# RWKV-7 mixer on one core: keys and bonus moved into the edge of a round, triangle and centring product placed later on TensorE, and the scan's state update made by ScalarE instead of VectorE

## The chip, the cores and the metric

The kernel runs on one core of one Trainium2 chip. The metric is the device time of one execution in microseconds (us), as the median of several runs. The engines are TensorE (PE in the views; PEld is its weight load), VectorE (DVE), ScalarE (ACT), GpSimd (POOL) and SyncE (SP, which issues the DMAs). Each works through its own queue in order, and they wait for one another by semaphores.

## What is computed

The program is the trunk of an encoder with two layers, 512 tokens and a width of 1024. Each layer has a token mixer (four heads of latent attention and eight heads of a bidirectional RWKV-7 recurrence, merged by one output projection) and a gated MLP. The change touches only the recurrence and what stands around it:

```python
def step(state, inp):
    r_t, w_t, k_t, v_t, kk_t, a_t = inp
    sa = jnp.einsum('bhvk,bhk->bhv', state, -kk_t)
    state = (state * w_t[:, :, None, :]
             + sa[..., None] * (kk_t * a_t)[:, :, None, :]
             + v_t[..., None] * k_t[:, :, None, :])
    y = jnp.einsum('bhvk,bhk->bhv', state, r_t)
    return state, y
...
def direction(xw, xa, d, reverse):
    w = rwkv_decay(xw, w0[d], w2[d])
    a = jax.nn.sigmoid(a0[d] + xa @ a2[d])
    k_d = k * (1 + (a - 1) * k_a)
    y = wkv7_scan(heads(r), heads(w), heads(k_d), heads(v), kk, heads(a), reverse)
    return y, k_d
...
y = y_f + y_b
mu = jnp.mean(y, axis=-1, keepdims=True)
var = jnp.mean(jnp.square(y - mu), axis=-1, keepdims=True)
y = ((y - mu) * lax.rsqrt(var + GN_EPS)).reshape(B, S, W) * gn_g + gn_b
k_bonus = 0.5 * (k_f + k_b)
bonus = jnp.sum(heads(r * k_bonus) * r_k, axis=-1, keepdims=True) * heads(v)
return (y.astype(r.dtype) + bonus.reshape(B, S, W)) * g
```

## The kernel before

The eight recurrent heads are worked in four blocks of two heads. A layer has five rounds (`rwkv_round`, called with cur = -1 to 3). Three blocks are in hand at a time. The round of block `cur` **scans** it; it **builds** block `cur + 1`, which means inverting its 64 x 64 triangular chunk matrices; it **trails** block `cur - 1`, which is the group norm, the gate and the bonus; and it prepares block `cur + 2` **early**, with its decays and rates. This text calls the four rounds that scan round 0 to round 3. Round 0 scans, builds and prepares, round 1 does all four, round 2 does everything except prepare, and round 3 scans and trails. Layer 0 has its scans at about 331 to 507 us of the span, layer 1 at about 1237 to 1412 us.

The 512 tokens of a block are 8 chunks of 64, and both time directions and both heads go together. So the scan has 8 **steps**, s = 0 to 7, each one passing from engine to engine and back:

- TensorE multiplies the state into the right side (`scan_state`, L640, then the reads L644 and the carry of the state L646, where the identity matrix copies it into the bank in which the update is added).
- ScalarE copies the right side out of PSUM (also named `scan_state`, L1103). Behind it comes the copy of the next chunk's tokens (`scan_ring`, L1098).
- TensorE **solves** with the inverse (`scan_solve`, L656), and then multiplies the Gram matrices of a later chunk (L603) and the values (L625).
- ScalarE copies the solution (`scan_solve`, L1110, two instructions of 64 partitions each).
- TensorE makes the state product (`scan_update`, L666) and the outputs (L672), and transposes the tokens of a later chunk (L615 to L618).
- VectorE multiplies the state product by the chunk's decay and writes the new state (`scan_state`, L1602). The next step's L640 waits for it.

```python
            def scan_state(it, s):

                dve.wait_ge(sc_p.sem, sc_p.at(f"S{s}", it))
                own(sc_v, TTT(SM[(s + 1) % 2], PS[1][:, 2 * P:3 * P].rearrange("p (d v) -> p d v", d=2),
                              EM[it % 2][:, :, s].unsqueeze(2).to_broadcast([P, 2, C]), ALU.mult), f"S{s}")
```

The order of each queue is written out by hand in the three functions `rwkv_round`, one for each engine, by the number of the step. The lists of step names (`sc_p`, `sc_a`, `sc_v`) turn a name into a semaphore value.

- TensorE has, at step 0, the second triangle of the block being built (L530, ahead of the state product) and the centring product of the trailing block (L680); at step 2 the variance product (L685), at step 3 the bonus product (L540), at step 4 the next block's decay product (L516), and at step 6 (step 4 in round 3) the gate (L690). The 512-wide ones each take TensorE for about the same time.
- ScalarE has, behind the solution copy of its step: the triangle copies (L1052, step 0); one inverse copy (L1061) and a table load with the square and the copy of the centred block (L961, L1123, L1124, step 1); the reversed values (L1045, step 2); a logarithm (L1133, step 3); three inverse copies (L1067, L1069, step 4); the next block's tanh (L1013, step 5); the norm's factor (L1138, step 6, in round 3 step 4) and the shift of the decays (L1019, step 6). In round 3 pairs of output copies (L1128) stand at steps 0, 2 and 5.
- VectorE has, behind the state update of its step, the masking of the Gram matrices (`scan_ring`, L1596) and a piece of the inverse. At step 0 both halves of `keys` (L1472 and L1474) and the inverse's transpose (L1507), at step 1 `bonus` (L1478, L1480), at step 4 `bonus_end` (L1485), at step 7 the group norm's end (`tail_norm`, L1609 to L1613), the decay sums (L1445) and the end of the inverse (L1575, L1577, L1585).

Between two scans lies the **edge**: the inverse is transposed and completed on TensorE and ScalarE in a chain of short products and copies (`rwkv_level`, L561 to L580, and `level`), while VectorE prepares the block after the next one (`queries`, `removals`). TensorE enters the edge only when VectorE's last reduction of the inverse (L1575) is done.

## Time and profile before

| | |
|---|---|
| median of 3 runs | 1866.26 us (1866.06 to 1869.93) |
| profiled execution: its time | 1867.6 us |
| profiled execution: its span | 1865.7 us |
| TensorE busy, share of the span | 1652.5 us, 89% |
| TensorE weight load | 1213.6 us, 65% |
| VectorE | 1007.7 us, 54% |
| ScalarE | 732.9 us, 39% |
| GpSimd | 289.4 us, 16% |
| mean granted TensorE clock | 0.939 |

The shares are means over stages with different limits. The chain of waits that ended last lies 57% on TensorE, 26% in TensorE's issue and other waits for nothing visible, 8% on VectorE and 4% on ScalarE. Outside the scans most of the span is TensorE's three-product matrix multiplications (L500 to L502). The clock is given as a share of the full 2.4 GHz: 1.00 is full speed, about 0.5 is the lower level of 1.2 GHz. In the timeline, times count from the start of the span; a bracket says how long the engine had stood idle before the instruction and for whom.

### The profile page before, as it was taken

The numbers are of one execution on the slowest core, as the hardware profiler recorded it, in microseconds if no ns is written. First come the engines' busy times: TensorE is split into PE (matmuls) and PEld (weight loads), VectorE is DVE, ScalarE is ACT, GpSimd is POOL, SyncE is SP. The second block draws the span as 40 slices with busy tenths as digits, with TensorE's granted clock in tenths as the row PEclk, the third lists the DMA queues.
The fourth block names the chain that finished last, engine by engine and source line by source line (L and its number), as shares of the span: only waits on it lengthen the run. The fifth ranks groups of instructions, "written<-read, shape, count | busy, mean of one in ns | idle before, by whom it ended". The sixth has DMA issues, their size and how long they took to land.

```text
span 1865.7 us, 28024 instructions
## 1 busy us (share of the span) xinstructions
PE 1652.5 (89%) x11272; PEld 1213.6 (65%) x11272; DVE 1007.7 (54%) x1533; ACT 732.9 (39%) x1201; POOL 289.4 (16%) x124
## 2 busy tenths in 40 slices
PE   2997866888998999989989978588889899999997
PEld 0784433666676888877757834266667688887885
DVE  6644558778217667754443244588752454445333
ACT  3434234665624232222233343456654422223223
POOL 1342000000032222211224400000002122222121
PEclk8998996989999999999989989789889999999999
DMA  7344110000043554443303210000002222222221
GB/s 294 135 161 158 47 75 1 2 2 2 2 147 118 198 191 180 180 158 135 129 9 124 91 68 1 0 2 2 2 2 91 68 90 90 97 105 90 77 103 68
DMA packets 34653, 163.00 MB, mean 87 GB/s; under 512 B 3840, under 2 KB 4096, under 8 KB 25856
## 3 DMA queue, kind: packets, MB, share of 16 engines
q1 hardware_dynamic: 34560, 161.65, 24.7%
q8 instruction: 71, 1.16, 0.3%
q14 instruction: 22, 0.18, 0.0%
HBM read 159.54 MB, written 2.10 MB: 87 GB/s over the span
## 4 chain that ended last, share of the span: by engine, by line
PE 57%; issue 26%; DVE 8%; ACT 4%; POOL 3%; DMA 1%; POOLq 0%; SPq 0%; DVEq 0%; ACTq 0%
PE bank L500 8%; PE bank L502 8%; PE bank L501 8%; PE bank_pair L500 3%; PE bank_pair L502 3%; PE bank_pair L501 3%; PE bank L547 2%; POOL work_parts L1925 2%; PE bank_pair L603 2%; PE bank L840 2%; PE bank L841 2%; PE bank L818 1%; PE bank L656 1%; POOL proj_weights_parts L1920 1%; PE bank L516 1%
## 5 line engine op out<-in xcount | busy, mean ns | idle before, releaser
L500 PE MATMUL bank<-work_parts,y_mix_parts 128*128 128x512 f32 x792 | 316.2, 399 | 21.4 <-DVE work_parts L1689 10.3
L502 PE MATMUL bank<-work_parts 128*128 128x512 f32 x792 | 315.3, 398 | 0.0
L1702 DVE TENSOR_TENSOR work_parts<-work,y_mix_parts 128x1024 fp32r<-128x1024 f32 x66 | 169.7, 2570 | 254.9 <-ACT y_mix_parts L970 254.9
L1920 POOL TENSOR_TENSOR proj_weights_parts<-proj_weights,proj_weights_hi_parts 128x1024 fp32r<-128x1024 f32 x54 | 130.1, 2416 | 934.1 <-ACT proj_weights_hi_parts L966 857.8
L1925 POOL TENSOR_TENSOR work_parts<-work,y_mix_parts 128x1024 fp32r<-128x1024 f32 x66 | 159.1, 2411 | 609.8 <-ACT y_mix_parts L970 609.8
L970 ACT ACTIVATE y_mix_parts<-work 128x1024 fp32r<-128x1024 f32 x132 | 133.0, 1054 | 261.1 <-DMA work<-mlp_dram 251.3
L501 PE MATMUL bank<-work_parts,y_mix_parts 128*128 128x512 f32 x528 | 208.4, 395 | 0.0
L500 PEld LDWEIGHTS bank<-work_parts,y_mix_parts 128*128 128x128 f32 x792 | 150.9, 190 | 59.1 <-issue 24.7
L502 PEld LDWEIGHTS bank<-work_parts 128*128 128x128 f32 x792 | 150.5, 190 | 35.8
L500 PE MATMUL bank<-work_parts,proj_weights_hi_parts 128*128 128x512 f32 x272 | 112.1, 412 | 26.2 <-DVE work_parts L1689 24.5
L501 PEld LDWEIGHTS bank<-work_parts,y_mix_parts 128*128 128x128 f32 x528 | 99.9, 189 | 24.1
L502 PE MATMUL bank<-work_parts,proj_weights_parts 128*128 128x512 f32 x272 | 109.0, 401 | 0.0
L501 PE MATMUL bank<-mixer_inputs_parts,y_mix_parts 128*128 (+1 forms) x264 | 105.3, 399 | 0.0
L502 PE MATMUL bank_pair<-work_parts 128*128 128x512 f32 x264 | 104.9, 397 | 0.0
L500 PE MATMUL bank_pair<-work_parts,y_mix_parts 128*128 128x512 f32 x264 | 104.4, 396 | 0.0
L1334 ACT ACTIVATE work<-work 128x512 f32<-128x512 f32 x44 | 27.8, 632 | 156.1 <-DVE work L1860 156.1
L1377 DVE CUSTOM_DVE_ANT_0 work<-work,c_act 128x1024 f32<-128x1024 f32 x64 | 77.6, 1249 | 12.1 <-DMA work<-ada_dram 12.1
L501 PE MATMUL bank<-work_parts,proj_weights_hi_parts 128*128 128x512 f32 x208 | 84.0, 404 | 0.0
L500 PEld LDWEIGHTS bank<-work_parts,proj_weights_hi_parts 128*128 128x128 f32 x272 | 52.4, 193 | 42.2 <-issue 27.3
L1602 DVE TENSOR_TENSOR rstd<-bank,chunk_ends 128x128 f32<-128x128 f32 x56 | 16.2, 289 | 103.4 <-PE bank L666 103.4
L500 PE MATMUL bank_pair<-work_parts,proj_weights_hi_parts 128*128 128x512 f32 x160 | 68.3, 427 | 3.9 <-POOL proj_weights_parts L1920 3.9
L501 PE MATMUL bank_pair<-work_parts,y_mix_parts 128*128 128x512 f32 x176 | 69.1, 393 | 0.0
(266 smaller groups left out, 3056.6 us busy)
## 6 DMA issues: line engine op xcount, KB each, us to landing
work<-mlp_dram SPq DMA_DIRECT2D x66, 1024.0 KB, 4.8
work<-ada_dram SPq DMA_DIRECT2D x64, 512.0 KB, 4.6
proj_weights<-tiles_dram SPq DMA_DIRECT2D x57, 512.0 KB, 3.6
x_res<-ada_dram SPq DMA_DIRECT2D x24, 512.0 KB, 4.9
x_res<-x_dram SPq DMA_DIRECT2D x2, 2048.0 KB, 10.6
mixer_inputs<-ada_dram SPq DMA_DIRECT2D x8, 512.0 KB, 17.8
work<-mlaw_dram SPq DMA_DIRECT2D x4, 640.0 KB, 4.5
out_dram<-x_res SPq DMA_DIRECT2D x8, 256.0 KB, 2.2
```

The lines of the kernel that those rows point to most:

```text
L500: mm(out, w_hi, x_hi, start=start, stop=False)
L501: mm(out, w_hi, x_lo, start=False, stop=False)
L502: return mm(out, w_lo, x_hi, start=False, stop=stop)
L547: mm(PS[1][:, :], ident, scan_mask, start=True, stop=True)
L603: last = mm(PS[3 + e][:, d * P:(d + 1) * P], BK[p][d][rows, s, :, :], ZR[p][d][rows, s, :, :], start=True, stop=True)
L840: mm(bank[:, :], QN[:, e, qb * P:(qb + 1) * P], KN[:, e, :], start=True, stop=False)
L841: mm(bank[:, :], QPE[:, qb * P:(qb + 1) * P], KPE[e], start=False, stop=True).then_inc(att_p.sem, att_p.one(f"sc{i}"))
L970: F(MW_H[q][:, half], MW_IN[q][:, half], ACT.Identity).then_inc(msp_a.sem, msp_a.one(f"h{half}"))
L1377: dve.tensor_tensor_reduce(out=slots[u], in0=slots[u], in1=CACT, scale=0.5, scalar=0.0, op0=ALU.mult, op1=ALU.add, accum_out=dots[:, u:u + ...
L1702: TTT(MW_L[q][:, 1], MW_IN[q][:, 1], plain(MW_H[q][:, 1]), ALU.subtract).then_inc(msp_v.sem, msp_v.one("l1"))
L1920: pool.tensor_tensor(ring_l[s], ring[s], plain(ring_h[s]), ALU.subtract).then_inc(spl_q.sem, spl_q.one(f"t{s}"))
L1925: pool.tensor_tensor(MW_L[q][:, 0], MW_IN[q][:, 0], plain(MW_H[q][:, 0]), ALU.subtract).then_inc(msp_q.sem, msp_q.one("l0"))
```

## The change

1. **State update.** VectorE's `scan_state` is gone. ScalarE has a function `scan_next` in its place: two ACTIVATEs, one for each time direction, of 128 partitions by 64, that read the same PSUM bank and take the decay as the scale operand, one column of 128 values. It stands right behind the solution copy of its step. TensorE's wait and the lists of step names follow.
2. **Triangle.** On TensorE the second triangle moves behind `scan_update` of step 0.
3. **Centring product.** It moves from the end of step 0 to step 1, between the state's products and the solve.
4. **Keys and bonus.** In VectorE's queue `keys` (both directions) and `bonus` move out of steps 0 and 1 to the end of the edge before, behind the second masking.

```diff
-        sc_a = steps("sc_a", ["T0", "R0", "SA0", "T1"] + [n for s in range(1, NCH) for n in [f"R{s}"] + ([f"T{s + 1}"] if s < NCH - 1 else []) + [f"SA{s}"]])
-        sc_v = steps("sc_v", ["G0", "G1"] + [n for s in range(NCH - 1) for n in [f"S{s}"] + ([f"G{s + 2}"] if s < NCH - 2 else [])])
+        sc_a = steps("sc_a", ["T0", "R0", "SA0", "S0", "T1"] + [n for s in range(1, NCH) for n in [f"R{s}"]
+                     + ([f"T{s + 1}", f"SA{s}", f"S{s}"] if s < NCH - 1 else [f"SA{s}"])])
+        sc_v = steps("sc_v", [f"G{s}" for s in range(NCH)])
...
@@ TensorE, scan_state
-                pe.wait_ge(sc_v.sem, sc_v.at(f"S{s - 1}", it))
+                pe.wait_ge(sc_a.sem, sc_a.at(f"S{s - 1}", it))
...
@@ TensorE, rwkv_round
                         if s:
                             scan_state(it, s)
+                        if trail and s == 1:
+                            if build:
+                                pe.wait_ge(tri_a.sem, tri_a.at("B10", new))
+                            tail_centre(old)
                         scan_solve(it, s)
...
+                        last = scan_update(it, s)
                         if s == 0 and build:
                             rwkv_triangle(new, 1)
-                        last = scan_update(it, s)
...
-                    if trail and s == 0:
-                        if build:
-                            pe.wait_ge(tri_a.sem, tri_a.at("B10", new))
-                        tail_centre(old)
...
@@ ScalarE
+            def scan_next(it, s):
+
+                if s == 0:
+                    act.wait_ge(pre_v.sem, pre_v.at("em1", it))
+                act.wait_ge(sc_p.sem, sc_p.at(f"S{s}", it))
+                for d in D2:
+                    last = F(SM[(s + 1) % 2][:, d, :], PS[1][:, 2 * P + d * C:2 * P + d * C + C], ACT.Identity, scale=EM[it % 2][:, d, s:s + 1])
+                own(sc_a, last, f"S{s}")
...
@@ ScalarE, rwkv_round
                     if scan:
                         scan_solve(it, s)
+                        if s < NCH - 1:
+                            scan_next(it, s)
...
@@ VectorE, rwkv_round
-                    if scan and s < NCH - 1:
-                        scan_state(it, s)
                     if scan and s < NCH - 2:
                         scan_ring(it, s + 2)
                     if build:
                         if s == 0:
-                            if scan:
-                                keys(new, nxt, 0)
                             inverse_in(new)
                             inverse_half(new)
-                            if scan:
-                                keys(new, nxt, 1)
                         if s == 1:
-                            if scan:
-                                bonus(new, nxt)
                             inverse_8(new, 1, 5)
...
                     scan_ring(new, 1)
+                    if early:
+                        for d in D2:
+                            keys(new + 1, nxt + 1, d)
+                        bonus(new + 1, nxt + 1)
```

Where the change moves instructions is seen best in two queues. In the rows below a line number of the changed kernel is up to 12 higher than that of the same code before.

ScalarE's queue at step 1 of round 1, before: the two solution copies (L1110), the inverse copy, the table load with its one-element ACTIVATE, the square and the copy of the centred block, and then the next step's copy of the right side (L1103).

```order
L1110 ACTIVATE work<-bank 64x2x64 [waits sc_p]
L1110 ACTIVATE work<-bank 64x2x64
L1061 ACTIVATE work<-work 64x16x16 [waits inv_v]
L961 ACT_TABLE_LOAD
L961 ACTIVATE spare<-constants 128x1
L1123 ACTIVATE squares<-bank 128x512 [waits tl_p]
L1124 ACTIVATE mixer_inputs<-bank 128x512
L1103 ACTIVATE rstd<-bank 128x128 [waits sc_p]
```

The same place in the changed kernel:

```order
L1111 ACTIVATE work<-bank 64x2x64 [waits sc_p]
L1111 ACTIVATE work<-bank 64x2x64
L1120 ACTIVATE rstd<-bank,chunk_ends 128x64 [waits sc_p]
L1120 ACTIVATE rstd<-bank,chunk_ends 128x64
L1062 ACTIVATE work<-work 64x16x16 [waits inv_v]
L962 ACT_TABLE_LOAD
L962 ACTIVATE spare<-constants 128x1
L1133 ACTIVATE squares<-bank 128x512 [waits tl_p]
L1134 ACTIVATE mixer_inputs<-bank 128x512
L1104 ACTIVATE rstd<-bank 128x128 [waits sc_p]
```

The two new ACTIVATEs wait for TensorE's state product, and everything that followed the solution copies now stands behind them.

VectorE's queue from the first state update of round 1 (L1602) to the beginning of the inverse's second piece, before:

```order
L1602 TENSOR_TENSOR rstd<-bank,chunk_ends 128x128 [waits sc_p]
L1596 TENSOR_TENSOR rstd<-bank_pair,constants 128x512 [waits sc_p]
L1472 TENSOR_TENSOR work<-work,mixer_inputs 128x512 [waits pre_a]
L1474 TENSOR_TENSOR work<-work 128x8x64 [waits pre_v]
L1507 STREAM_TRANSPOSE work<-work 64x1024 [waits tri_a]
L1512 COPY work<-work 64x16x16 [waits inv_v]
L1472 TENSOR_TENSOR work<-work,mixer_inputs 128x512 [waits pre_a]
L1474 TENSOR_TENSOR work<-work 128x8x64 [waits pre_v]
L1602 TENSOR_TENSOR rstd<-bank,chunk_ends 128x128 [waits sc_p]
L1596 TENSOR_TENSOR work<-bank_pair,constants 128x512 [waits sc_p]
L1478 TENSOR_TENSOR work<-work 128x512
L1480 SCALAR_TENSOR_TENSOR work<-work,derived,mixer_inputs 128x512 [waits bon_v]
```

The same stretch in the changed kernel, from the end of the edge on:

```order
L1608 TENSOR_TENSOR work<-bank_pair,constants 128x512 [waits sc_p]
L1484 TENSOR_TENSOR work<-work,mixer_inputs 128x512 [waits pre_a]
L1486 TENSOR_TENSOR work<-work 128x8x64 [waits pre_v]
L1484 TENSOR_TENSOR work<-work,mixer_inputs 128x512 [waits pre_a]
L1486 TENSOR_TENSOR work<-work 128x8x64 [waits pre_v]
L1490 TENSOR_TENSOR work<-work 128x512
L1492 SCALAR_TENSOR_TENSOR work<-work,derived,mixer_inputs 128x512 [waits bon_v]
L1608 TENSOR_TENSOR rstd<-bank_pair,constants 128x512 [waits sc_p]
L1519 STREAM_TRANSPOSE work<-work 64x1024 [waits tri_a]
L1524 COPY work<-work 64x16x16 [waits inv_v]
L1608 TENSOR_TENSOR work<-bank_pair,constants 128x512 [waits sc_p]
L1530 COPY lane_inverse<-work 128x2 [waits inv_v]
```

The six instructions of keys and bonus now stand ahead of the scan's first masking, and both state updates are gone.

## Rows read from the trace of the kernel before

**Rows 1.** Windows, the scans: stretch length, PE PEld DVE ACT POOL busy, PEclk, DMA, GB/s.

```profile
280.00:508.50 228.50, 191.92 (x3129) 136.16 (x3130) 160.80 (x287) 130.75 (x276) 0.00 (x0) 0.86 0.01 2
1186.00:1412.00 226.00, 186.43 (x3124) 132.65 (x3125) 165.24 (x297) 131.75 (x277) 0.00 (x0) 0.87 0.01 2
```

**Rows 2.** Idle time of VectorE ahead of L1602: releaser, us, times.

```profile
  PE bank L666: 103.4, 41
```

**Rows 3.** Timeline, layer 0, round 2, step 4: start, us, engine, line, op.

```profile
448.27 0.45 PE L656 MATMUL bank<-rstd,work 64*64 64x64 f32 x8
449.34 0.41 ACT L1067 ACTIVATE lane_inverse<-lane_inverse 64x256 f32<-64x256 f32 x1
449.78 1.31 ACT L1069 ACTIVATE work<-lane_inverse 64x256 f32<-64x256 f32 x2
449.57 0.40 PE L666 MATMUL bank<-work 128*64 128x64 f32 x8
450.02 0.29 DVE L1602 TENSOR_TENSOR rstd<-bank,chunk_ends 128x128 f32<-128x128 f32 x1 [1.39 <-PE bank L666]
450.73 0.45 PE L640 MATMUL bank<-rstd,work 64*64 64x64 f32 x8
451.22 0.28 ACT L1103 ACTIVATE rstd<-bank 128x128 f32<-128x128 f32 x1
451.76 0.45 PE L656 MATMUL bank<-rstd,work 64*64 64x64 f32 x8
```

**Rows 4.** Timeline, layer 0, round 1, step 1.

```profile
386.66 0.41 ACT L1061 ACTIVATE work<-work 64x256 f32<-64x256 f32 x1
387.09 1.28 ACT L961 ACT_TABLE_LOAD   x1
389.09 0.59 ACT L1124 ACTIVATE mixer_inputs<-bank 128x512 f32<-128x512 f32 x1
389.57 0.28 ACT L1103 ACTIVATE rstd<-bank 128x128 f32<-128x128 f32 x1
389.91 0.45 PE L656 MATMUL bank<-rstd,work 64*64 64x64 f32 x8 [0.36 <-ACT rstd L1103]
```

**Rows 5.** Timeline, layer 0, round 2: its first state update.

```profile
432.21 0.29 DVE L1602 TENSOR_TENSOR rstd<-bank,chunk_ends 128x128 f32<-128x128 f32 x1 [4.65 <-PE bank L666]
```

**Rows 6.** Groups by form, ScalarE: count, busy us, mean ns, idle before.

```profile
L1103 ACT ACTIVATE rstd<-bank 128x128 f32<-128x128 f32 x64 | 17.8, 278 | 74.8 <-PE bank L640 74.3
L1098 ACT ACTIVATE work<-bank 128x512 f32<-128x512 f32 x64 | 38.0, 593 | 5.6 <-PE bank L618 5.4
L1194 ACT ACTIVATE mixer_inputs<-bank,derived 128x512 f32<-128x512 f32 x20 | 13.8, 690 | 18.5 <-PE bank L502 18.5
```

**Rows 7.** Round 0, step 1 of both layers, and the window behind layer 1's.

```profile
341.07 0.45 PE L640 MATMUL bank<-rstd,work 64*64 64x64 f32 x8 [1.35 <-DVE rstd L1602]
1245.72 0.45 PE L640 MATMUL bank<-rstd,work 64*64 64x64 f32 x8 [1.61 <-DVE rstd L1602]
1246.75:1250.30 3.55, 3.55 (x43) 3.09 (x43) 2.61 (x11) 1.29 (x4) 0.00 (x0) 0.52 0.01 2
```

**Rows 8.** Timeline, layer 0, round 1, step 4.

```profile
401.90 1.13 PE L516 MATMUL bank<-mixer_inputs 64*128 64x512 f32 x4 [0.77 <-DVE y_mix L1485]
```

**Rows 9.** Timeline, layer 0, end of round 2, and last the end of round 0.

```profile
456.35 0.45 PE L666 MATMUL bank<-work 128*64 128x64 f32 x8 [0.28 <-ACT work L1110]
456.32 1.28 ACT L1138 ACT_TABLE_LOAD   x1
457.61 0.63 ACT L1138 ACTIVATE squares<-squares 128x512 f32<-128x512 f32 x1
458.79 0.74 DVE L1609 SCALAR_TENSOR_TENSOR squares<-mixer_inputs,params,squares 128x512 f32<-128x512 f32 x1
462.82 0.48 PE L615 MATMUL bank<-constants,work 128*128 128x128 f32 x1 [1.77 <-DVE lane_inverse L1575]
362.39 2.33 DVE L1445 TENSOR_TENSOR_SCAN work<-constants,work 128x512 f32<-128x512 f32 x2
```

4 lines of the change are left out of this document (removed).

## Prediction

> **What bounds it now.** I read the windows view first: the two scan stages take 228.5 and 226.0 us, with TensorE busy for 192 and 186 us of them [rows 1]. Only these stages are touched. Then the wait totals: VectorE stands idle 103.4 us ahead of the state update, for TensorE's product [rows 2]. In an in-order queue its inverse pieces wait along.
>
> Then one plain step in the timeline [rows 3]. All times below count from the solve (448.27). The next solve is at 3.49. ScalarE is free of the solution copy at 1.07, its other work, which I call the **rest**, ends at 2.82 (451.09), and it copies the right side at 2.95. The state product starts at 1.30, VectorE's update runs from 1.75 to 2.04, and L640 starts at 2.46, when TensorE's own queue lets it. So a plain step is TensorE's queue, with ScalarE and VectorE just inside it. A 512-wide product in the step adds some 0.87 (4.35 in all), which the other two get as slack.
>
> It is different where the rest is long. At step 1 of round 1 it runs from 386.66 to 389.57, 2.91 us, and the solve follows 0.34 after that copy, TensorE having waited 0.36 for ScalarE [rows 4]. So the step's length is the larger of TensorE's queue (3.49 or 4.35) and 1.07 + rest + 0.34. Here that gives 4.32.
>
> **State update on ScalarE.** It adds 56 pairs of ACTIVATEs, 128x64 from PSUM with a column as scale, a form that the trace lacks. From 128x128 at 278 ns and 128x512 at 593 ns a 64-column one is 226 ns, and the column operand adds 97 ns (690 against 593) [rows 6]. Neighbours overlap by 0.11 (389.09 + 0.59 against 389.57) [rows 4]. So a pair takes 2 x 0.323 - 0.11 = 0.53 us. Bounds: 0.34 if the column costs nothing, 0.65 without overlap. I take 0.53, as both effects have a row. The Trainium skill's page "ScalarE: Activation LUTs" (section "What ACT_TABLE_LOAD costs") gives 186 ns plus 0.833 ns an element plus 93 ns a pointer operand and a like overlap, so a pair of 0.57 us as an estimate, which would add under 1 us to the sum below.
>
> The pair starts at 1.75 and ends at 2.28. L640 could follow at once, still before 2.46: a plain step stays 3.49. But ScalarE comes to its rest at 2.28 where it was 1.07, **1.21 us later**. The new length is the larger of TensorE's queue and 2.28 + rest + 0.34, so rest over 0.87 us (over 1.7 in a 4.35 step) now costs. By round, for one layer:
>
> - Round 1: step 1, ScalarE was already late: +1.2. Step 5 has a table load of 1.28 and two 512-wide ACTIVATEs, rest 2.43, also late already: +1.2.
> - Round 2: step 1 +1.2. Step 4, rest 1.75: 4.37 against 3.49, +0.9.
> - Round 3: step 1 +1.2; step 4, rest 1.8 in a 4.35 step, +0.1; step 5, rest 1.05, 3.67 against 3.49, +0.2; step 6, where no Gram product fills TensorE, 0.53 in place of 0.29, +0.2.
> - Round 0: step 5, two ACTIVATEs (1.15), 3.77 against 3.49, +0.3.
> - Steps 2 and 3 have a 512-wide product and a short rest: nothing.
>
> **What VectorE gives back.** In round 0 step 1 L640 waits 1.35 us (layer 0) and 1.61 us (layer 1) for an update that stands behind the keys [rows 7]: both go. After the second, the window shows a clock of 0.52, the level of 1.2 GHz, for 3.55 us, and that step 2 takes 4.92 (solves at 1246.75 and 1251.67) instead of about 3.57: 1.35 us more goes, if the fall does. In rounds 0 and 1 at step 4 the decay product waits 0.77 for `bonus_end` [rows 8], which stands behind an update that itself waited 1.39 in the like step [rows 3]: -0.8 each.
>
> Round ends: TensorE enters the edge when VectorE has its last reduction (L615 waits 1.77 us for L1575) [rows 9]; what ScalarE costs at step 6 of rounds 0 to 2 counts only through this. In round 2 the group norm (458.79) began 0.55 after its factor was ready (457.61 + 0.63 = 458.24). Now the pair runs from 456.35 + 0.45 to 457.33, the load and factor (1.92) end at 459.25, and VectorE starts 0.5 later: +0.5. In round 1 no load precedes the factor and VectorE was the late one by some 0.6: -0.6. In round 0 the decay sums (362.39, 3.54 after that step's solve at 358.85) wait for the first shift, 2.08 + 0.61 after the solve: -0.8.
>
> **The moves.** Keys and bonus are six 512-wide operations of about 0.7 us (0.74 in rows 9), 4.2 us. VectorE stood idle 4.65 us there, waiting for the first product [rows 5], and longer in the other rounds, so they hide; without that cover the first masking would come late by the difference. The triangle and the centring product keep their length and only change places in a queue that TensorE works through anyway: 0 for both, between -0.3 (the copies run under the product) and +0.24 (the state product now waits for the solution copy without a triangle in front) a round. No DMA moves.
>
> **Sum for a layer.** Round 0: -1.35 - 0.8 + 0.3 - 0.8 = -2.65 in layer 0, and in layer 1 -1.6 - 1.35 - 0.8 + 0.3 - 0.8 = -4.25. Round 1: 1.2 + 1.2 - 0.8 - 0.6 = +1.0. Round 2: 1.2 + 0.9 + 0.5 = +2.6. Round 3: +1.7. So +2.65 and +1.05, together +3.7.
>
> **The clock.** In step 1 of rounds 1 to 3 TensorE will stand still for 5.53 - 3.49 = 2.04 us before the solve. Of the two waits in rows 7, 1.61 was followed by a fall and 1.35 was not. A fall costs 1.35 as in layer 1; six places give bounds of 0 and 8.1. I take two of six, 2.7: the wait is longer than the one that was followed by a fall, but unlike there TensorE is at full work on both sides of it, its queue being refilled by the centring product. In all +6.4 us: the profiled execution would be 1867.6 + 6.4 = 1874.0. It lies 1.3 above the median of the runs, so against that the forecast is 1872.7.
>
> **Rivals.**
> - *Same.* The pair takes 0.34 and the clock holds. The pair's length enters at about 11 places a layer, 0.19 each: 3.7 - 4.2 = -0.5, so 1865.8 to 1870. For it: the margin is small against 56 updates. Against it: the 97 ns of the column operand stand in two forms of ScalarE's rows. 0.24.
> - *The clock falls at all six places* [rows 7]: 1866.26 + 3.7 + 8.1 = 1878.1. For it: the new wait is longer than the one that was followed by a fall. 0.15.
> - *Faster: VectorE's queue was the true limit.* If ScalarE's rest were no obstacle to the next right side (place: L1103 behind the table load, deciding from a rest of 0.87 us), only the gains stay: round 0 -2.9 and -4.55, round 1 -1.4 in each layer, round 2 -0.6 in each: -11.5, 1854.8; with half of ScalarE's 15.2 us of costs 1862.4. For it: the 103.4 us of idle time [rows 2]. Against it: most of that idle time costs nothing, and rows 4 show ScalarE late with 1.2 us less in front. 0.15.
> - That the change doesn't do what it says is ruled out by the queues shown above.
>
> **How the numbers follow.** A measurement here can tell 0.2%, 3.7 us, from no change. The forecast (1870 to 1877) has 0.46, the clock rival 0.15, same 0.24, faster 0.15; all of the first two count as slower, 0.61 less a sliver that lands under 1870, so 0.60, with 0.25 same and 0.15 faster. The range is 1862 to 1880: below it lies most of the faster rival; above, the clock rival together with a pair of 0.65 (+2.6).
>
> **What would show it.** Right: L1120 at about 0.53 a pair; ScalarE the releaser of the solve at step 1 of rounds 1 to 3, with TensorE waiting near 2 us; step 1 near 5.5; no wait of L640 in round 0; the decay product's wait at step 4 gone; round 2 and 3 longer by 2 to 3 us each and round 0 shorter by as much. Wrong: a pair under 0.4; the solve of step 1 still at 4.3; rounds 1 to 3 no longer than before, or the edge longer because the keys reach into the scan.

## The result, and the profile after

The changed kernel takes 1876.25 us (median of 7 runs, 1872.45 to 1883.29), the kernel before 1866.26 us (7 runs). The ratio is 1.0067, with a 95% interval of 1.0047 to 1.0086: **slower**, as forecast, by 10.0 us where 6.4 were forecast. Its profiled execution took 1874.33 us with a span of 1872.4 us, 6.7 us more than before; the traces below explain these 6.7 us. Four of the seven runs lie at 1872 to 1876 us with a mean granted clock of 0.938 to 0.940, the other three at 1881.5 to 1883.3 us with 0.933.

The first and fourth part of the changed kernel's page: busy time of each engine, and the chain that ended last.

```profile
PE 1653.5 (88%) x11272; PEld 1212.1 (65%) x11272; DVE 997.2 (53%) x1477; ACT 757.1 (40%) x1313; POOL 289.2 (15%) x124
...
PE 58%; issue 25%; DVE 6%; ACT 5%; POOL 3%; DMA 1%; POOLq 0%; SPq 0%; DVEq 0%; ACTq 0%
```

ScalarE gained 24.2 us of busy time, VectorE lost 10.5, TensorE's is 1.0 us off. So the totals show the move of the work and nothing of its price. The windows from the first solve to the last of each layer, and the stretch between the layers, of the changed kernel (columns as in [rows 1]):

```profile
328.96:508.40 179.44, 157.74 (x2682) 115.01 (x2682) 112.89 (x186) 115.37 (x283) 0.00 (x0) 0.90 0.01 2
508.40:1239.97 731.57, 665.77 (x2946) 490.02 (x2947) 381.44 (x556) 255.57 (x364) 145.12 (x60) 0.95 0.31 110
1239.97:1416.62 176.65, 155.03 (x2683) 113.68 (x2683) 113.70 (x188) 115.27 (x283) 0.00 (x0) 0.91 0.01 2
```

The same three stretches of the kernel before:

```profile
331.16:505.36 174.20, 155.39 (x2682) 115.33 (x2682) 118.24 (x215) 103.17 (x227) 0.00 (x0) 0.91 0.01 2
505.36:1237.06 731.70, 666.49 (x2946) 490.45 (x2947) 382.15 (x557) 255.69 (x364) 145.26 (x60) 0.95 0.31 110
1237.06:1410.15 173.09, 154.07 (x2683) 114.01 (x2683) 118.43 (x215) 103.03 (x227) 0.00 (x0) 0.92 0.01 2
```

The scans of layer 0 are 5.2 us longer and those of layer 1 3.6; between the layers nothing changed (731.57 against 731.70). The first solve comes 2.2 us earlier and the last stretch is 0.2 longer, which makes 6.7.

The next table cuts the scans at the starts of the solves (L656 before, L657 after), in us. A step is the stretch from its own solve to the next one; the last column but one goes from the last solve of a round to the first of the next, and so holds step 7 and the edge.

| | step 0 | 1 | 2 | 3 | 4 | 5 | 6 | edge | sum |
|---|---|---|---|---|---|---|---|---|---|
| layer 0, round 0, before | 6.03 | 4.91 | 3.53 | 4.35 | 5.38 | 3.49 | 2.77 | 16.35 | 46.81 |
| after | 4.80 | 3.49 | 3.49 | 4.35 | 4.57 | 3.65 | 3.56 | 15.53 | 43.44 |
| round 1, before | 7.61 | 4.33 | 4.34 | 4.35 | 5.39 | 3.85 | 3.60 | 18.22 | 51.69 |
| after | 6.98 | 5.43 | 5.94 | 4.35 | 4.58 | 5.07 | 4.71 | 15.60 | 52.66 |
| round 2, before | 5.38 | 4.53 | 4.35 | 4.35 | 3.49 | 3.49 | 3.60 | 17.05 | 46.24 |
| after | 5.66 | 5.43 | 5.93 | 4.35 | 4.21 | 3.49 | 4.29 | 17.01 | 50.37 |
| round 3, before | 7.13 | 3.88 | 4.35 | 3.49 | 4.35 | 3.49 | 2.77 | | 29.46 |
| after | 8.87 | 5.30 | 4.35 | 3.49 | 4.43 | 3.53 | 3.00 | | 32.97 |

Layer 1 gives for its four rounds -4.24, +1.17, +3.14 and +3.49 us. The same steps move, except that step 2 of its round 2 stays at 4.35.

**The step that ScalarE sets.** Timeline of the changed kernel, layer 0, round 1, from the solve that begins step 1 to the next one; it answers to [rows 4].

```profile
379.38 0.45 PE L657 MATMUL bank<-rstd,work 64*64 64x64 f32 x8
381.14 0.52 ACT L1120 ACTIVATE rstd<-bank,chunk_ends 128x64 f32<-128x64 f32 x2 [0.70 <-PE bank L667]
381.68 0.41 ACT L1062 ACTIVATE work<-work 64x256 f32<-64x256 f32 x1
382.12 1.28 ACT L962 ACT_TABLE_LOAD   x1
...
383.52 0.58 ACT L1133 ACTIVATE squares<-bank 128x512 f32<-128x512 f32 x1
384.00 0.59 ACT L1134 ACTIVATE mixer_inputs<-bank 128x512 f32<-128x512 f32 x1
384.47 0.28 ACT L1104 ACTIVATE rstd<-bank 128x128 f32<-128x128 f32 x1
384.81 0.39 PE L657 MATMUL bank<-rstd,work 64*64 64x64 f32 x6 [1.87 <-ACT rstd L1104]
```

The pair (L1120) takes 0.52 us and stands ahead of the inverse copy, the table load and the two 512-wide copies. The right side is copied at 384.47, 5.09 after the solve, and the next solve follows 0.34 later, TensorE having stood idle for 1.87 us where it was 0.36 in [rows 4]. The same form in ScalarE's groups, and then what L1120 waited for and who waited for it (us, times):

```profile
L1120 ACT ACTIVATE rstd<-bank,chunk_ends 128x64 f32<-128x64 f32 x112 | 29.1, 311 | 40.9 <-PE bank L667 40.9
```

```profile
  PE bank L667: 40.9, 56
  PEld bank L641: 10.2, 30
  PE bank L641: 1.5, 4
```

The 112 instructions take 29.1 us together. The totals show 24.2 more: 3.3 of the 29.1 overlap with ScalarE's other instructions, and those take 1.6 less than before. Nobody waits much for the pair itself: 11.7 us in 34 places, 0.34 us each. The larger waits are for what stands behind it.

**The gains.** L641 in round 0 and the decay product in round 1 start without a bracket, which answers to [rows 7, 8]:

```profile
336.22 0.45 PE L641 MATMUL bank<-rstd,work 64*64 64x64 f32 x8
397.59 1.13 PE L517 MATMUL bank<-mixer_inputs 64*128 64x512 f32 x4
```

**The clock.** Windows over step 2 of rounds 1 and 2, layer 0 and then layer 1, of the changed kernel:

```profile
386.40:389.70 3.30, 3.30 (x22) 1.83 (x18) 2.92 (x9) 1.04 (x3) 0.00 (x0) 0.53 0.00 0
437.60:441.00 3.40, 3.40 (x26) 2.09 (x22) 3.07 (x9) 1.04 (x3) 0.00 (x0) 0.54 0.00 0
1294.00:1297.40 3.40, 3.40 (x24) 1.84 (x20) 3.08 (x9) 1.04 (x3) 0.00 (x0) 0.51 0.00 0
1346.60:1350.80 4.20, 4.20 (x64) 3.06 (x64) 2.90 (x9) 2.40 (x8) 0.00 (x0) 1.00 0.02 4
```

After the wait of step 1 the granted clock was 0.53, 0.54 and 0.51, the level of 1.2 GHz, in three places and 1.00 in the fourth. Step 2 took 5.92 to 5.94 us in those three and 4.35 in the fourth, so a fall costs 1.58 us. Round 3 has a shorter wait, 1.43 us in both layers (its step 1 takes 5.30 and 5.14 us), and no fall.

**What I had not foreseen.** Timeline of the changed kernel, layer 0, step 0 of round 3:

```profile
478.00 0.52 ACT L1120 ACTIVATE rstd<-bank,chunk_ends 128x64 f32<-128x64 f32 x2 [1.29 <-PE bank L667]
478.41 0.60 ACT L1099 ACTIVATE work<-bank 128x512 f32<-128x512 f32 x1
478.89 1.16 ACT L1138 ACTIVATE work_parts<-y_mix 128x512 fp32r<-128x512 f32 x2
479.15 0.69 PE L626 MATMUL bank<-work 128*64 128x64 f32 x8 [0.83 <-ACT work L1099]
482.46 1.91 PE L681 MATMUL bank<-squares,constants 128*128 128x512 f32 x2
484.30 0.69 PE L657 MATMUL bank<-rstd,work 64*64 64x64 f32 x8
```

The same products in the kernel before, the values product without a wait:

```profile
478.58 0.64 PE L625 MATMUL bank<-work 128*64 128x64 f32 x8
480.06 1.92 PE L680 MATMUL bank<-squares,constants 128*128 128x512 f32 x2
```

The copy of the tokens (L1099) stood right behind the solution copy before and now stands behind the state update, and the values product (L626) waits 0.83 us for it. In the other rounds the triangle, moved to just this place, covers that; round 3 has no triangle. Step 0 takes 8.87 us against 7.13 (in layer 1 8.88 against 7.00). About 1.0 of the added 1.75 us lies ahead of the values product. Another 0.6 lies behind it: the granted clock over the step is 0.50 against 0.56 before, so the reads and the carry of the state run at 1.2 GHz here (0.64 and 0.79 us), where they took 0.40 and 0.49 in the kernel before. The centring product (L681) adds nothing by its new place, as it took 1.92 us before too.

**The end of round 2**, which answers to [rows 9]:

```profile
458.31 0.75 DVE L1615 SCALAR_TENSOR_TENSOR squares<-mixer_inputs,params,squares 128x512 f32<-128x512 f32 x1 [1.71 <-ACT squares L1148]
...
460.49 1.80 DVE L1587 TENSOR_REDUCE lane_inverse<-work 128x64 f32<-128x512 f32 x2
462.35 0.69 PE L616 MATMUL bank<-constants,work 128*128 128x128 f32 x2 [1.73 <-DVE lane_inverse L1587]
```

The norm (L1615) begins 4.18 us after the solve of step 6 (454.13), where it was 3.54 before; the inverse's reduction (L1587) stands behind it, and TensorE waits 1.73 us for that (1.77 before). So VectorE and TensorE are both later by 0.6 us.

### The profile page after: what moved, and what is told of

Its sections match the earlier page's. It is cut to its first block, busy times and chain, and to the rows that moved or that the text cites. A ratio compares the mean times of both kernels' runs of the same rounds, so it can differ in the third digit from the quotient of the medians.

```text
span 1872.4 us, 28088 instructions
## 1 busy us (share of the span) xinstructions
PE 1653.5 (88%) x11272; PEld 1212.1 (65%) x11272; DVE 997.2 (53%) x1477; ACT 757.1 (40%) x1313; POOL 289.2 (15%) x124
## 4 chain that ended last, share of the span: by engine, by line
PE 58%; issue 25%; DVE 6%; ACT 5%; POOL 3%; DMA 1%; POOLq 0%; SPq 0%; DVEq 0%; ACTq 0%
PE bank L501 8%; PE bank L503 8%; PE bank L502 7%; PE bank_pair L501 3%; PE bank_pair L503 3%; PE bank_pair L502 3%; PE bank_pair L604 2%; POOL work_parts L1927 2%; PE bank L548 2%; PE bank L841 2%; PE bank L842 2%; PE bank L819 1%; PE bank L657 1%; PE bank L626 1%; PE bank L517 1%
## 5 line engine op out<-in xcount | busy, mean ns | idle before, releaser
L502 PEld LDWEIGHTS bank<-work_parts,y_mix_parts 128*128 128x128 f32 x528 | 100.1, 190 | 24.2
L1608 DVE TENSOR_TENSOR work<-bank_pair,constants 128x512 f32<-128x512 f32 x48 | 32.8, 684 | 72.2 <-PE bank_pair L604 72.1
```

The costliest lines, as they stand in the source:

```text
L502: mm(out, w_hi, x_lo, start=False, stop=False)
```

## The experiments

A run names its theory by a letter in the expectations below: A is the prediction's, that the rest in ScalarE's queue sets the length; B, that the new places of triangle and centring product cost; C, that the clock alone does; D, that step 2 is long for another reason or its falls are chance; E, that only the pair's own length counts; F, that it is the wait for the bonus product itself; G, that the gain needs the products' moves too; H, that the edge waits for the transpose anyway. Ratios are to the kernel before, measured on the same chip at the same time, with the 95% interval. The first four, as they stand here, share one chip; e5, e6, e7 and e8 share a second, e10, e3 and e9 a third; e11 was measured on a fourth.

### The changed kernel again (a1_changed_again)

> The changed kernel beside its parts, on their chip. Theory A (ScalarE's queue: the state update stands ahead of everything ScalarE does between two copies of the right side) and rival B (the places of the triangle and the centring product cost the time) both expect what was measured, 1872 to 1884 us, since how often TensorE's clock falls after its wait at step 1 changes from execution to execution.

1887.47 us (4 runs), 1.0125 (1.0107 to 1.0144). That is above the first measurement's interval. Its scans take 355.1 us together, against 356.1 in the first trace; the falls at step 2 are four, not three, step 0 of round 3 is 8.88 twice. The span is 5.9 us longer, and that lies outside the scans: the first solve is 3.6 us later and the stretch between the layers 3.5 longer, at a mean clock of 0.935 against 0.939. So the price in the scans repeats to 1 us, and the whole time does so only to 0.6%.

### The moves without ScalarE (e1_moves_only)

```diff
 (against the changed kernel; the lists of step names and the function `scan_state` are as before)
-                pe.wait_ge(sc_a.sem, sc_a.at(f"S{s - 1}", it))
+                pe.wait_ge(sc_v.sem, sc_v.at(f"S{s - 1}", it))
...
-                        if s < NCH - 1:
-                            scan_next(it, s)
...
+                    if scan and s < NCH - 1:
+                        scan_state(it, s)
```

> Triangle, centring product, keys and bonus as in the changed kernel, state update back on VectorE. Theory A: only the gains stay, so 1856 to 1861 us, step 1 of rounds 1 to 3 back at 4.3 us and no fall of the clock behind it. Rival B: the products' new places cost what was seen, so 1868 or more, with step 1 still above 5 us.

1861.15 us (12 runs), 0.9983 (0.9965 to 1.0001). Two rows of its timeline, layer 0, round 1: the solve at the end of step 1, and the decay product at step 4.

```profile
384.07 0.45 PE L656 MATMUL bank<-rstd,work 64*64 64x64 f32 x8 [0.77 <-ACT rstd L1103]
396.06 1.13 PE L516 MATMUL bank<-mixer_inputs 64*128 64x512 f32 x4 [0.77 <-DVE y_mix L1485]
```

Step 1 of rounds 1 to 3 is at 4.33, 4.33 and 3.88, none longer than before, and in round 0 it is 3.49: the keys' gain is there. Step 2 is 4.35 at all six places. But the decay product still waits 0.77 us and step 4 stays 5.39: that gain needs the update off VectorE's queue, or something else ahead of `bonus_end`. Step 0 of round 3 takes 6.69 and 6.64 us, so the products' new places cost nothing there with VectorE's update. Step 0 of round 2 in layer 0, at a clock of 1.00 in both kernels, is 5.60 where it was 5.38. B falls as a cause of its own. In the whole time the gain isn't clear of the noise, as the interval reaches 1.

### ScalarE without the other moves (e2_act_only)

```diff
 (against the kernel before; scan_next, the step names and TensorE's wait as in the change)
-                    if scan and s < NCH - 1:
-                        scan_state(it, s)
...
+                        if s < NCH - 1:
+                            scan_next(it, s)
```

> Only the state update moves to ScalarE; keys, bonus, triangle and centring product stay where they were. Theory A: slower than the kernel before by 10 us or more and not faster than the changed kernel: 1876 to 1884 us. Rival B: without the moves nothing is lost, so 1862 to 1868 us.

1894.3 us (5 runs), 1.0154 (1.0131 to 1.0177). The solve at the end of step 1, layer 0, round 1:

```profile
395.72 0.68 PE L657 MATMUL bank<-rstd,work 64*64 64x64 f32 x8 [1.86 <-ACT rstd L1104]
```

The expected 1876 to 1884 us were too low by 10 us or more. The wait is 1.86 us with the centring product in its old place, and step 1 takes 5.42. So the queue behind the pair sets that length, whatever TensorE does around it. Step 2 is long at four of six places. Here round 0 gains at steps 1 and 4 as well (3.48 and 4.58), although keys and bonus stand in their old places: with no state update behind them they hold up nobody. The median is above the changed kernel's on the same chip (1887.47), though the intervals overlap: that the products' moves cost the time is excluded here too.

Step 0 shows more. The values product of round 3, and then that of round 2, both in layer 0:

```profile
492.64 0.70 PE L626 MATMUL bank<-work 128*64 128x64 f32 x8 [0.83 <-ACT work L1099]
441.90 0.45 PE L626 MATMUL bank<-work 128*64 128x64 f32 x8 [1.02 <-ACT work L1099]
```

Step 0 of round 3 takes 8.88 and 8.44 us here as well, so its cost comes with ScalarE's update and needs none of the products' moves. And the token copy is now late in every round, since the triangle stands ahead of the state product and covers nothing: step 0 of round 2 is 6.62 us in layer 0, against 5.38 in the kernel before and 5.66 in the changed one, where L626 starts without a wait. The difference is the same in round 0 of layer 1 (5.76 against 4.81). So behind ScalarE's update the triangle's new place is worth 1.0 us a round in rounds 0 to 2.

### Tokens ahead of the state update (e4_tokens_first, against the changed kernel)

```diff
-        sc_a = steps("sc_a", ["T0", "R0", "SA0", "S0", "T1"] + [n for s in range(1, NCH) for n in [f"R{s}"]
+        sc_a = steps("sc_a", ["T0", "R0", "SA0", "T1", "S0"] + [n for s in range(1, NCH) for n in [f"R{s}"]
...
+                        if s == 0:
+                            scan_ring(it, 1)
                         if s < NCH - 1:
                             scan_next(it, s)
-                    if scan and s == 0:
-                        scan_ring(it, 1)
```

> The changed kernel with ScalarE's copy of the next tokens (T1) put ahead of the new state update at step 0. Theory A, refined: in round 3, where no triangle stands between, TensorE's values product waits 0.83 us for this copy while its clock is low; step 0 of round 3 goes from 8.9 us back toward 7.2, 1.5 us a layer, 3 us in all. Rival C: the 8.9 us are the clock's alone and step 0 stays above 8.5, no change in the time.

1874.93 us (6 runs), 1.0067 (1.0042 to 1.0091). The same stretch of its timeline as shown above of the changed kernel, layer 0, step 0 of round 3:

```profile
478.55 0.60 ACT L1099 ACTIVATE work<-bank 128x512 f32<-128x512 f32 x1
479.82 0.52 ACT L1120 ACTIVATE rstd<-bank,chunk_ends 128x64 f32<-128x64 f32 x2 [0.67 <-PE bank L667]
479.92 0.64 PE L626 MATMUL bank<-work 128*64 128x64 f32 x8
483.04 1.02 PE L681 MATMUL bank<-squares,constants 128*128 128x512 f32 x2
483.99 0.45 PE L657 MATMUL bank<-rstd,work 64*64 64x64 f32 x8
```

The tokens are copied first, L626 starts without a wait, the clock rises within the step (0.51 over 477.24 to 483.00, 1.00 over the next microsecond) and the centring product takes 1.02 us. Step 0 is 6.75 and 6.88 us where it was 8.87 and 8.88, and the missed term is gone. But step 2 of round 3, 4.35 in the changed kernel, is now 5.87 and 5.88, after the same wait of 1.43 us that no fall followed there, and falls follow the wait of step 1 at four of six places. About three quarters of what is saved at step 0 is given back there. Its interval lies below that of the changed kernel on the same chip and nearly equals that of the changed kernel's first measurement, so what it is worth in the whole time stays open.

### A cheap pair (e6_cheap_pair, against the changed kernel)

```diff
-                for d in D2:
-                    last = F(SM[(s + 1) % 2][:, d, :], PS[1][:, 2 * P + d * C:2 * P + d * C + C], ACT.Identity, scale=EM[it % 2][:, d, s:s + 1])
-                own(sc_a, last, f"S{s}")
+                own(sc_a, F(SM[(s + 1) % 2].rearrange("p d v -> p (d v)"), PS[1][:, 2 * P:3 * P], ACT.Identity, scale=0.0), f"S{s}")
```

> The changed kernel with one ACTIVATE of 128x128 and a constant scale of 0 in place of the pair: the state between chunks is left out (written as zero), all instructions else stay. Theory A: 0.28 us instead of 0.52 on ScalarE, so step 1 of rounds 1 to 3 goes from 5.43 to 5.19, step 4 of round 2 from 4.21 to 3.97, and about 11 places a layer give 5 us in all; still slower than the kernel before. Rival E (the pair's own length is the cost, the wait in front of it is not): step 1 back near 4.3 + 0.28 and the time within 3 us of the kernel before.

This kernel leaves out the state between chunks: one ACTIVATE writes it as zero. 1875.56 us (6 runs), 1.0059 (1.0038 to 1.0081). Timeline, layer 0, round 1, step 1:

```profile
377.49 0.28 ACT L1119 ACTIVATE rstd<-bank 128x128 f32<-128x128 f32 x1 [0.70 <-PE bank L667]
...
380.92 0.45 PE L657 MATMUL bank<-rstd,work 64*64 64x64 f32 x8 [1.62 <-ACT rstd L1104]
```

The one instruction takes 0.28 us in place of 0.52. Step 1 takes 5.18 us, 0.25 less; step 4 of round 2 3.97 against 4.21, step 5 of round 1 4.83 against 5.07. Each ScalarE-bound step of rounds 1 and 2 moves by the difference of the pair's length and by nothing more. Step 1 is still 0.85 us over its 4.33 before, and only 0.28 of that is the instruction. The rest is ScalarE's wait from the solution copy until the state product is there (0.70 us in the first row, less some 0.1 by which the rest has become shorter), which now stands ahead of everything else. In the whole time the 5 us that theory A expected don't show: the scans of its trace take 354.5 us against 356.1, since step 0 and the edges are longer in it. It has one fall at step 2.

### A pair that waits for nothing (e7_extra_pair)

```diff
 (against the kernel before)
+        scratch = sb("scratch", 2 * C)
...
+                        if s < NCH - 1:
+                            for d in D2:
+                                F(scratch[:, d * C:d * C + C], CST[:, d * C:d * C + C], ACT.Identity, scale=ones[:, 0:1])
```

> The kernel before (state update on VectorE) with an extra pair of ACTIVATEs, 128x64 with a column as scale, behind each solution copy, into a scratch tile; it waits for nothing new. It separates ScalarE's occupation (0.52 us) from its wait for the state product (0.7 us). Theory A: only the places where ScalarE was late grow, step 1 of rounds 1 to 3 and step 5 of round 1 by 0.5 each instead of 1.1 to 1.2, steps 2 and 3 unchanged: 5 to 8 us slower than before, with fewer falls of the clock than in the changed kernel. Rival E: the full cost of the change, 1.1 us at step 1.

1873.46 us (12 runs), 1.004 (1.002 to 1.006). Timeline, layer 0, round 1, step 1:

```profile
388.51 0.57 ACT L1154 ACTIVATE scratch<-constants 128x64 f32<-128x64 f32 x2
...
392.34 0.45 PE L657 MATMUL bank<-rstd,work 64*64 64x64 f32 x8 [1.23 <-ACT rstd L1104]
```

The pair runs at once behind the solution copy, and step 1 takes 4.79 us: 0.46 more than before, against 1.10 with the real one. In step 1 the occupation is less than half of the price and the wait for TensorE's product the larger part. E falls. Behind step 1 of rounds 1 to 3, where TensorE waits 0.4 to 1.2 us, the clock doesn't fall at any of the six places.

### Filling the wait (e5_act_fill, e10_fill_step2)

```diff
 (e5_act_fill, against the changed kernel: ahead of the solve of s = 1)
                             tail_centre(old)
+                            if build:
+                                pe.wait_ge(tri_a.sem, tri_a.at("B11", new))
+                            for _ in range(2):
+                                mm(PS[6][:, :], ident, scan_mask, start=True, stop=True)
```

> The changed kernel with two products of the identity, 512 wide, on TensorE at step 1 of rounds 1 to 3, where it waits 1.4 to 1.9 us for ScalarE. Theory A with the clock as its second part: the 1.74 us of products fit into the wait, step 1 stays near 5.4, and step 2 is 4.35 at all six places instead of 5.9 at half of them; 5 to 8 us faster than the changed kernel, ratio to the kernel before about 1.004. Rival D (step 2 is long for another reason, the falls are chance): step 2 still at 5.9 in three or four places and the time as it was, or longer by the products.

1892.82 us (5 runs), 1.0156 (1.0134 to 1.0178). I had put the products one solve too early: they lie in step 0, where TensorE had no idle time, and lengthen it from 6.98 to 8.69 and from 5.66 to 7.38 us in layer 0, while the wait of step 1 keeps its 1.86 us. It tells nothing of the fill. The same four lines ahead of the solve of s = 2:

> The changed kernel with the two products of the identity moved to where TensorE's wait in fact lies, behind the state's products of step 2 and ahead of its solve (in the earlier try they stood ahead of the solve of step 1, where TensorE had no time to spare). Theory A with the clock: the 1.74 us fit into the wait of 1.4 to 1.9 us, so step 1 stays at 5.4 to 5.5 and step 2 is 4.35 at all or nearly all six places of rounds 1 to 3; 3 to 6 us faster than the changed kernel, ratio about 1.004 to 1.007. Rival D: step 2 still at 5.9 in half of the places and the time not better.

1877.64 us (10 runs), 1.0063 (1.0037 to 1.009). Timeline, layer 0, round 1, the fill and the solve behind it, and then windows over the step 2 that follows, in rounds 1 and 2:

```profile
386.00 1.88 PE L709 MATMUL bank<-constants 128*128 128x512 f32 x4
388.03 0.45 PE L657 MATMUL bank<-rstd,work 64*64 64x64 f32 x8
```

```profile
388.00:392.40 4.40, 4.37 (x66) 3.17 (x66) 2.99 (x9) 2.60 (x8) 0.00 (x0) 1.00 0.00 0
439.97:444.30 4.33, 4.33 (x64) 3.15 (x64) 2.94 (x9) 2.53 (x8) 0.00 (x0) 1.00 0.00 0
```

The fill takes the 1.88 us of the wait, the solve comes no later (step 1 5.42), the clock stays at 1.00, and step 2 is 4.35 us at all six places of this one trace. So the falls at step 2 were caused by TensorE's standing still, and D falls. What it is worth in the whole time stays open: the ratio is 1.0063, against the changed kernel's 1.0067 in one measurement and 1.0125 in the other, each on another chip or at another time. In its trace the scans take 355.3 us against 356.1. Of the 4.7 us saved at step 2 most is found again in step 0 and in the edges (step 0 of round 0 6.16 against 4.80, the edge of round 1 17.53 against 15.60 and 18.26 against 16.43). Whether the fill causes this or the execution fell so, this pair of traces can't tell.

### Bonus ahead, keys alone (e8_bonus_first, e3_keys_only)

```diff
 (e8_bonus_first, against e1_moves_only, on VectorE)
+                    if build and s == 4:
+                        bonus_end(new, nxt)
                     if scan and s < NCH - 1:
                         scan_state(it, s)
...
                         if s == 4:
-                            bonus_end(new, nxt)
                             inverse_32_first(new)
```

> State update on VectorE with the moves of the change, and the end of the bonus put ahead of the state update of step 4 in VectorE's queue. Theory A: TensorE's wait of 0.77 us ahead of the next block's decay product comes from VectorE's in-order queue, so step 4 of rounds 0 and 1 goes from 5.39 to about 4.6; 3 us faster than the moves alone, about 1858 us, 0.4% faster than the kernel before. Rival F: the wait is for the bonus product itself, step 4 stays at 5.39 and nothing is won.

1863.72 us (12 runs), 0.9985 (0.9967 to 1.0002). Step 4 of rounds 0 and 1 takes 4.55 us in both layers (5.39 before). So the 0.8 us of the change at that step can be had with VectorE's update, by the order of two calls, and F falls. The 3 us expected of it in the whole time don't show: the ratio of the moves alone was 0.9983.

The next kernel is the kernel before with only keys and bonus moved to the edge:

```diff
 (e3_keys_only, against the kernel before; the calls at steps 0 and 1 go as in the change)
                     scan_ring(new, 1)
+                    if early:
+                        for d in D2:
+                            keys(new + 1, nxt + 1, d)
+                        bonus(new + 1, nxt + 1)
```

> The kernel before with only keys and bonus moved into the edge. Theory A: the gain of the moves is this part's; step 1 of round 0 goes from 4.9 and 5.2 to 3.49 and step 2 of layer 1 to 3.49, rounds 1 and 2 hardly change; as fast as all moves together, 1859 to 1863 us. Rival G: the gain needs the triangle and the centring product behind the state product too; then step 1 stays above 4 and the time at 1865.

1862.32 us (12 runs), 0.9986 (0.9968 to 1.0003). Step 1 of round 0 takes 3.49 us in both layers, and no step 1 to 6 of any round is longer than before: the whole gain of round 0's step 1 is the keys', and neither ScalarE nor the products are needed for it. G falls. In its trace the scans are 13.4 us shorter than before (333.9 against 347.3), but everything outside them, where the edit changes no work of TensorE, is 9.7 us longer; so the whole time tells little of what the edit is worth.

### The inverse ahead of the norm (e9_inverse_before_norm, e11_inverse_only)

```diff
 (e9_inverse_before_norm, against e8_bonus_first, on VectorE at s == 7)
+                            if not early:
+                                inverse_32_end(new)
+                                inverse_out(new)
                             if trail:
                                 tail_norm(old, cur - 1)
                             if early:
...
-                            inverse_32_end(new)
-                            inverse_out(new)
+                                inverse_32_end(new)
+                                inverse_out(new)
```

> The moves with the bonus's end first, and in round 2 the end of the inverse put ahead of the group norm in VectorE's queue. TensorE enters the edge of that round when VectorE's last reduction is done, and waits 1.8 us for it; the norm's three operations (2.2 us) stand in front. Theory A: the edge of round 2 gets 1.5 to 2 us shorter in each layer, 3 to 4 us in all, about 1856 to 1860 us. Rival H: the edge then waits for the transpose and ScalarE's chain all the same, and its length stays within 0.5 us.

**1851.2 us** (6 runs), 0.9922 (0.99 to 0.9944): faster than both kernels, and by 5 to 9 us more than was expected. Its timeline, layer 0, end of round 2, against [rows 9]:

```profile
455.26 1.81 DVE L1575 TENSOR_REDUCE lane_inverse<-work 128x64 f32<-128x512 f32 x2
...
459.57 0.70 DVE L1609 SCALAR_TENSOR_TENSOR squares<-mixer_inputs,params,squares 128x512 f32<-128x512 f32 x1
457.45 0.44 PE L615 MATMUL bank<-constants,work 128*128 128x128 f32 x2
```

The reduction starts at 455.26, right behind the multiply that it needs, and TensorE enters the edge at 457.45 without a wait. The edge of round 2 takes 13.92 and 13.43 us in place of 17.05 and 15.96. H falls.

The same edit on the kernel before, alone:

> The kernel before with only the last edit of e9_inverse_before_norm: in round 2 VectorE does the end of the inverse ahead of the group norm, in place of behind it. If what counts is the wait of TensorE at the entry of the edge, the edge of round 2 falls from 17.05 and 15.96 us to about 13.9 and 13.4 as in e9, nothing else moves, and the time is 5.7 us below the kernel before, near 1860.5, a ratio of 0.997. If the whole distance between e9 and e8 (1851.2 against 1863.7, 12.5 us) belongs to this edit, because the shorter wait also leaves the clock higher afterwards, the ratio is near 0.993. If e9 gains only together with the keys' new place, the edge stays within 1 us of the kernel before.

1862.23 us (12 runs) against 1867.01, 0.9972 (0.9959 to 0.9984). The edge of round 2 is 13.95 and 13.38 us, as expected; 4.8 us were gained where 5.7 were expected. So this edit carries about a third of the 14.1 us by which e9_inverse_before_norm is below its 1865.3. The moves together with the earlier `bonus_end` (e8_bonus_first) came to 1.5 us on another chip. The parts fall short of the whole by some 8 us. The traces of the scans don't show this: there e8_bonus_first is 7.8 us below the kernel before, e11_inverse_only 7.5 and e9_inverse_before_norm 12.7. So the shortfall isn't in the scans of these traces, and where it comes from is not settled.

## Why the prediction was right, point by point

- **What bounds it now.** Right. The larger of TensorE's queue and 2.28 + rest + 0.34 gave 5.53 us for step 1 of rounds 1 and 2; it measured 5.43. For step 4 of round 2 it gave 4.37 and 4.21 was measured; for step 5 of round 1 5.05 and 5.07; for step 5 of round 0 3.77 and 3.65. The missing 0.1 at step 1 is the rest itself, 2.79 us (381.68 to 384.47) in place of 2.91. In steps 2 and 3 the pair costs nothing, as said: without a fall they are 4.35.
- **State update on ScalarE.** The pair was taken at 0.53 from rows of other forms and measured 0.52: 311 ns each, with an overlap of 0.10. An estimate from the Trainium skill's page "ScalarE: Activation LUTs" (section "What ACT_TABLE_LOAD costs") is 332 ns for one and 0.57 for the pair; the measurement lies a little below it.
- **What VectorE gives back.** Right: round 0 gained 3.37 and 4.24 us (2.65 and 4.25 forecast), step 4 of rounds 0 and 1 0.8 each. The 0.8 forecast for the end of round 0 came in layer 1, where step 6 and the edge together are 0.77 shorter. In layer 0 they are 0.03 shorter, and step 0 is 1.23 us shorter instead, for which the forecast had no term. That length also moves with the clock (6.03 and 4.52 in the two layers of the kernel before), so that the sum of layer 0 comes near is partly luck. Part of the reasoning was too narrow, since e3_keys_only and e2_act_only each have the gain of step 1 by themselves.
- **Round ends.** Round 2 was forecast at +2.6 and is +2.6 and +3.1 without its fall. Round 1 was forecast at +1.0 and is -0.6 and -0.4 without its fall: step 6 and the edge together are 1.5 and 2.0 us shorter, where I had taken 0.6. The edge of round 1 ranges from 15.6 to 20.6 us over these kernels, and I can't say which part of it is the change.
- **The step that failed: step 0 of round 3.** The list by rounds under "State update on ScalarE" has no term for it; it is +1.74 and +1.88 us. I had listed what stands behind the pair for steps with a long rest, and left out the one copy at step 0 that TensorE needs before the next solve: the token copy stands behind the state update in ScalarE's queue and the values product behind the token copy in TensorE's, in a stretch at 1.2 GHz. e4_tokens_first removes this wait. Without that step round 3 is +1.77 and +1.61, with +1.7 forecast.
- **The moves.** I wrote that triangle and centring product only change places, 0 for both, and no more than 0.24 a round. At full clock step 0 of round 2 is longer by 0.22 us with the moves alone (5.60 against 5.38) and by 0.28 in the changed kernel (5.66), which is at the upper bound. But the reason given was incomplete. Behind ScalarE's update the triangle's new place covers the late token copy, without which step 0 would be 1.0 us longer in rounds 0 to 2 (e2_act_only). The error of round 3 belongs to the state update, since e2_act_only, with the products in their old places, has it too.
- **The clock.** That the wait brings the falls is shown, by the fill in e10_fill_step2, but both factors were too small: three falls of 1.58 us, 4.7 us, in place of two of 1.35, 2.7. The second trace has four. TensorE's wait was 1.87 us in rounds 1 and 2 and 1.43 in round 3, where 2.04 was forecast for all.
- **The sum.** Of the 6.7 us of span, +4.1 are the scans without the falls (+3.7 forecast), +4.7 the falls (+2.7), and -2.1 lie outside the scans, where I had 0. The two errors of the scans, +3.6 in round 3 and about -3.0 in round 1, cancel. So the forecast of the profiled execution, 1874.0 against 1874.33, is closer than its parts deserve, and that is luck. The median lies 3.6 us above the forecast, because the changed kernel's runs spread upward at lower clocks.
- **The rivals.** "Same" with a cheap pair: the pair isn't cheap (0.52), and e6_cheap_pair, with 0.28, is still slower. In its trace the scans are 7.2 us over those of the kernel before; 2.8 of them are step 0 of round 3 (8.31 and 8.64), which neither I nor this rival had counted, and 1.6 are one fall. "VectorE's queue was the true limit": the solve of step 1 waits 1.87 us for ScalarE, so ScalarE's rest is the obstacle that this rival denied, and in rounds 1 to 3 VectorE's idle time ahead of the update bought nothing there. "The clock falls at all six places": three and four of six in the two traces of the changed kernel.

## What to carry to other kernels

Moving a short instruction to another engine moves its wait as well: here 0.52 us of work put 1.2 us in front of everything behind it in an in-order queue, so price the step by what stands behind the moved instruction, down to the smallest copy that another engine needs, before looking at busy totals. An edit that carries several moves should be taken apart, since here the ones worth having (keys in the edge, `bonus_end` ahead, and the inverse ahead of the norm) needed none of the costly one. Each of the three shortens its own steps in the traces; in the whole time only the last is clear of the noise by itself. Moves can also belong together: the products' new places cost 0.2 us at step 0 with VectorE's update, and with ScalarE's the triangle's saves 1.0. Where an engine enters the next stage on the last item of another engine's queue, ask which items ahead of it could as well follow.

## What the runs showed of the hardware

- A stretch of 1.2 GHz followed TensorE's standing still for 1.87 us at three of four like places (rounds 1 and 2) in one execution of the changed kernel and at all four in another, and costs 1.58 us of a 4.35 us step. The 1.43 us in round 3, where step 0 had run at a clock of 0.50, were followed by none in these two traces; in e4_tokens_first, where step 0 of round 3 ended at 1.00, both were followed by one. Filling the wait with products left no fall in the one trace taken; whether it shortens the whole time is open.
- For the changed kernel the time of an execution goes with its mean granted clock: it ran in 1872.45 us at 0.940 and in 1889.92 us at 0.929. Two kernels with the same code up to round 2, e8_bonus_first and e9_inverse_before_norm, have their first solve at 336.80 and 331.06 us, with a clock of 0.60 and 0.65 from 280 to 330 us. What lies outside the scans, where these edits hardly change the work, took from 1516.1 us (e4_tokens_first) to 1529.4 us (e2_act_only) over the fourteen traces. So the whole span of a single profiled execution can be off by more than this change's price. The steps inside the scans that the clock leaves alone agree to 0.02 us from trace to trace.
- The table load of step 1 takes 1.28 us, and the next ACTIVATE starts 0.01 us later (383.41, with the load from 382.12), so that the switch costs 1.3 us here. The same section of the Trainium skill's page "ScalarE: Activation LUTs" puts a switch at about 2.66 us with the drain in it; the trace doesn't agree, and an estimate by that figure would have made each step 1 of rounds 1 to 3 some 1.4 us longer than measured.
